# Moving vector-engine work in a transformer kernel: the context half's low parts, and the scalings of four attention heads

## What is computed

```
# end of the first block: the embedding gate
e = sigmoid(x @ w_ple_gate) * (p @ w_ple_proj)
x = x + rmsnorm(e, ple_post_norm)

# start of the second block, layer 0
xn = modulate(rmsnorm_2(h,  norm_mix), sh_m,  sc_m)     # latent half, h = x
xc = modulate(rmsnorm_2(hc, norm_mix), csh_m, csc_m)    # context half
# differential attention over both halves, per head
p = softmax(q1 k1) - lam * softmax(q2 k2);  o = p @ v
o = rmsnorm_2(o, subln) * (1 - lam_init);   y = o @ wo
```

## Time and profile before

| | before |
|---|---|
| median of 3 runs | 1462.05 us |
| profiled execution | 1463.88 us |
| its span | 1462.1 us |
| PE busy | 1411.9 us (97%) |
| DVE busy | 707.8 us (48%) |
| ACT busy | 610.8 us (42%) |
| POOL busy | 854.7 us (58%) |

### The profile page before, as it was taken

The page is one execution under the profiler, slowest core; times in us unless marked ns, Lnnn a source line. Parts: engine busy times, 40 slices in busy tenths (PEclk is TensorE's granted clock), DMA queues, the critical chain, the costliest instruction groups (busy, mean ns, idle before and its releaser), DMA issues.

```text
span 1462.1 us, 25892 instructions
## 1 busy us (share of the span) xinstructions
PE 1411.9 (97%) x9196; PEld 1262.4 (86%) x9196; DVE 707.8 (48%) x1315; ACT 610.8 (42%) x976; POOL 854.7 (58%) x426
## 2 busy tenths in 40 slices
PE   8999999999899999699999999999999999999998
PEld 7998999999787888577888888888888788999997
DVE  5884555555625556635655655334324383311111
ACT  6346544544533444534322322322332265444452
POOL 4785688798455766241443543544374452688895
PEclk8999999999899999899999999999999999999999
DMA  7653477785322223021565565635293101455563
GB/s 292 228 151 123 177 269 273 283 303 190 123 87 69 76 73 102 1 91 54 201 209 191 178 213 183 217 130 175 69 263 114 45 5 64 135 185 184 176 210 106
DMA packets 82971, 227.27 MB, mean 155 GB/s; under 512 B 23648, under 2 KB 29024, under 8 KB 82656
## 3 DMA queue, kind: packets, MB, share of 16 engines
q1 hardware_dynamic: 82464, 224.91, 45.6%
q10 hardware_dynamic: 448, 1.57, 0.5%
HBM read 222.26 MB, written 1.05 MB: 153 GB/s over the span
## 4 chain that ended last, share of the span: by engine, by line
issue 36%; PE 32%; POOL 27%; DVE 2%; ACT 1%; POOLq 1%; DVEq 0%; ACTq 0%
POOL wl L528 24%; PE ps L1045 7%; PE ps L1047 7%; PE ps L1046 7%; PE ps L1118 1%; PE ps L1132 1%; PE ps L1108 1%; PE ps L1109 1%; PE ps L1110 1%; PE ps L1382 1%; POOL xl L562 1%; PE ps L1308 1%; PE ps L1329 1%; PE ps L1396 1%; PE ps L1374 1%
## 5 line engine op out<-in xcount | busy, mean ns | idle before, releaser
L528 POOL TENSOR_TENSOR wl<-raw,wh 128x1024 fp32r<-128x1024 f32 x310 | 743.4, 2419 | 542.0 <-ACT wh L632 541.9
L1045 PE MATMUL ps<-xh,wh 128*128 128x256 f32 (+1 forms) x1728 | 561.4, 325 | 10.5 <-POOL wl L528 2.9
L1046 PE MATMUL ps<-xl,wh 128*128 128x256 f32 (+1 forms) x1728 | 555.1, 321 | 0.0
L1047 PE MATMUL ps<-xh,wl 128*128 128x256 f32 (+1 forms) x1728 | 554.8, 321 | 0.0
L632 ACT ACTIVATE wh<-raw 128x1024 fp32r<-128x1024 f32 x310 | 318.2, 1053 | 283.4 <-PE ps L1047 194.7
L1045 PEld LDWEIGHTS ps<-xh,wh 128*128 128x128 f32 x1728 | 330.7, 191 | 43.7 <-POOL wl L528 5.2
L1047 PEld LDWEIGHTS ps<-xh,wl 128*128 128x128 f32 x1728 | 330.5, 191 | 24.1
L1046 PEld LDWEIGHTS ps<-xl,wh 128*128 128x128 f32 x1728 | 330.9, 191 | 22.4
L1045 PE MATMUL ps<-fh,wh 128*128 128x256 f32 (+1 forms) x528 | 168.8, 320 | 1.7 <-POOL wl L528 1.7
L1046 PE MATMUL ps<-fl,wh 128*128 128x256 f32 (+1 forms) x528 | 168.6, 319 | 0.0
L1047 PE MATMUL ps<-fh,wl 128*128 128x256 f32 (+1 forms) x528 | 168.6, 319 | 0.0
(11 more groups left out here) (223 smaller groups left out, 1663.3 us busy)
## 6 DMA issues: line engine op xcount, KB each, us to landing
raw<-wall SPq DMA_DIRECT2D x310, 512.0 KB, 3.7
ada_late<-wada SPq DMA_DIRECT2D x56, 512.0 KB, 3.4
ada<-wada SPq DMA_DIRECT2D x40, 512.0 KB, 3.7
bias<-rpb SPq DMA_DIRECT2D x16, 256.0 KB, 6.2
h<-xin SPq DMA_DIRECT2D x2, 1024.0 KB, 7.2
sww<-qk SPq DMA_DIRECT2D x16, 128.0 KB, 2.3
csb<-cond SPq DMA_DIRECT2D x1, 1024.0 KB, 8.2
sw<-u ACTq DMA_DIRECT2D x2, 512.0 KB, 6.7
```

Source lines behind the costliest of these rows:

```text
L528: nc.gpsimd.tensor_tensor(wl[:, slot, :, :], raw[:, slot, :, :], wh[:, slot, :, :].bitcast(F32), ALU.subtract).then_inc(lo_ready, 1)
L1045: nc.tensor.matmul(o, wa, xa, start=start, stop=False, skip_group_check=True)
L1046: nc.tensor.matmul(o, wa, xb, start=False, stop=False, skip_group_check=True)
L1047: return nc.tensor.matmul(o, wb, xa, start=False, stop=stop, skip_group_check=True)
```

## The change

It moves DVE's instructions alone; the other four engines' programs are the same.

```diff
                 V.tensor_tensor(ppo[:, 2 * p:2 * p + 2, :], ppo[:, 2 * p:2 * p + 2, :], pair_banks(p % 2, SEQ), ALU.mult)\
                     .then_inc(bank_free, 1)
-                modulate_part(0, 1, CTX_TILES[p] if p < 3 else (), CTX_TILES[p - 1] if p else (), yc)
+                modulate_part(0, 1, CTX_TILES[p] if p < 3 else (), {1: CTX_TILES[0], 3: CTX_TILES[1]}.get(p, ()), yc)
             recip("ple1", SEQ)
             add_normed(ppo, par_ap("ple_post"))
+            modulate_part(0, 1, (), CTX_TILES[2], yc)
...
-                    def out_scaled(b):
+                    def out_scaled(b, tiles):
...
-                        dve.wait_ge(S("da_root"), b + 1)
-                        link(V.reciprocal(part, part))
-                        link(V.tensor_scalar(part, part, 1.0 - LAM_INIT, None, ALU.mult))
-                        for t in range(4):
+                        if 0 in tiles:
+                            dve.wait_ge(S("da_root"), b + 1)
+                            link(V.reciprocal(part, part))
+                            link(V.tensor_scalar(part, part, 1.0 - LAM_INIT, None, ALU.mult))
+                        for t in tiles:
...
                         combine(w)
-                        if w == 16:
-                            out_scaled(0)
                     for w in range(WOVEN, ATT0 + 5):
...
+                        if WOVEN < w <= WOVEN + 4:
+                            out_scaled(0, (w - WOVEN - 1,))
                         if w - 5 >= WOVEN:
                             squares(w - 5)
 
                     out_low(0)
-                    out_scaled(1)
+                    out_scaled(1, range(4))
```

## The result

The changed kernel took 1455.51 us (median of 6 runs, 1452.23 to 1458.34) against 1462.74 us before (6 runs). The measured ratio is 0.9944, 95% interval 0.9931 to 0.9956, so 8.2 us less; it is not the quotient of the two medians, which lie 7.2 us apart. A second set of runs later gave 1453.24 us and 0.9925 (0.9912 to 0.9938), 11.0 us less (10.4 by the medians). The forecast was 8.75 us less and 1453.3 us. The span of the profiled execution went from 1462.1 to 1453.1.

The account below looks back on a forecast made before the run. PE was taken to be bound by two waits for DVE, 4.82 us in the gate and 6.83 us in the attention. A -3.15 and B -5.6 sum to -8.75: 1462.05 to 1453.3 us, range 1449.8 to 1457.9.

Parts of the forecast that it names:

- A: Gate: DVE's add for the sum of squares starts earlier, PE's sums follow; -3.15 us, bounds -2.5 and -4.5.
- B: Attention: the sum of B1 to B4, -5.6 us.
- The clock, which I had as a rival with 0.18: Gate: granted clock stays high behind the shorter idle, A becomes -4.5, 1452.0 us in all; chance 0.18.
- B1: Attention: group 17's maxima start at once after its scores, so its turn comes earlier; -6.6 us, bounds -6.8 and -5.5.
- B2: Attention: without PE's long idle, group 17's turn and scores run at a higher clock; -1.2 us, bounds -1.2 and 0.
- B3: Attention, group 18: a small DVE instruction on the chain may wait for POOL; +0.65 us, bounds 0 and +1.3.
- B4: Last six groups: moved work costs 3.0 us less 1.45 us of idle; +1.55 us, bounds 0 and +3.0.
- the clock in the last groups: Rival: clock stays low over all six last groups as PE waits longer; +3.2 us, 1465.2; chance 0.03.
- The weights: Rival: the weight stream sets the pace behind the gate, A and part of B go; about 1461 us; chance 0.04.

Follow-up runs that it names:

- e1: Gate's part of the change alone, attention as before, against the kernel before: 0.9969, -4.5 us.
- e2: Attention's part of the change alone, gate as before, against the kernel before: 0.9973, -3.9 us.
- e5: Kernel before plus 30 filler matmuls on PE ahead of the sums of the gate's norm, DVE's order old: 0.9994 of before.
- e8: Changed kernel with e3's and e4's rearrangements and a second filler between the columns of the norm m0's sums: 0.9898 of before, 1448.80 us.
- e10: Changed kernel with e3's and e4's rearrangements together, a repeat run of that kernel: 0.9906 of before.
- e4: Changed kernel with the four scalings of heads 0 to 3 in steps 24 to 27 instead of 19 to 22: 0.9921 of before.
- e3: Changed kernel with the copy of the last projection pair ahead of group 18's maxima instead of behind them: 0.9920 of before.
- e9: Changed kernel with filler matmuls on PE ahead of its wait for the combines of groups 18, 19 and 22: 0.9916 of before.
- e6: Changed kernel with all scalings of heads 0 to 3 in step 17, behind group 17's maxima: 0.9959 of before.
- e11: e8's kernel with e9's fillers in the last groups added: 0.9906 of before, 1450.62 us.

## Why the prediction came out as it did

The time was right, and both mechanisms are shown: each of the two long waits of PE went (to 1.58 and 0.81 us), and each part alone gives its share (e1, e2). That the number came so near is in part luck: A came out 1.4 us larger than forecast in the two profiles compared above and B 2.0 us smaller, and the granted clock is behind much of both.

*A, the gate.* The order gave 3.25 us (product of pair 1 to the add: 14.64 before, 11.39 after) where I had 3.15. The clock, which I had as a rival with 0.18, held high in this place and added 1.82 at the reciprocal; e5 gives the same 1.83 by itself, though its time did not fall with it. Of the 11 profiles with the changed gate 9 show it; e8 and e10 reach the reciprocal at 16.48 and 16.77 us instead of 15.4. At the reciprocal of the norm m0 the gain was 5.51 us, of which 0.9 was given back by group 16's turn: layer 0's first products now ran in a low stretch (394.5 to 401.4). From the one profile before, A is -4.58 to -4.98 in ten of the 11 profiles and -3.05 in e10, not -3.15; and e2, with the old order, is itself 1.2 us longer than that profile.

*B1.* The maxima of group 17 came 6.64 us earlier (-6.6 forecast). From their start to the end of the combine it took 7.45 us and not 6.83, mostly because one small instruction (L1820) took 1.20 us beside POOL (0.34 before); the turn came 6.01 earlier.

*B2.* Turn and scores at the high clock: -1.15 (-1.2 forecast).

*B3* was off in size: +1.28 instead of +0.65. The wait that I forecast came as forecast: L1804 took 0.77 us beside POOL instead of 0.17, and e4, which has the same order here and a high clock, is 0.60 longer than before (4.22 against 3.62). The other 0.68 is a term that I left out: the clock fell at 585.7, and from the start of group 19's scores to its maxima it took 1.69 us, in e4 1.01. The copy L1793, for which PE idled 2.17 us, is not a cost of its own. It stood behind the small instruction before, too; PE now only came to wait for it earlier. It can be taken out of the way, as e3 shows.

*B4:* +2.23 instead of +1.55. The products took 0.68 to 0.69 us each, as forecast. The idle time of 1.45 us that I set against 3.0 us of work was still there in part (0.77 before group 22's maxima): the wait for scores moved along with the chain. And part of the 2.23, up to 0.9 by e9, is the clock again; e4 takes back the whole, scalings and clock together.

B was -3.65 and not -5.6; A and B together -8.2 and not -8.75. I had the clock in the last groups only as a rival in which it stays low over all six, and no term for its falling over a part of them, as it did in the changed kernel (585.7 to 589.1 and 592.5 to 599.3). The weights took nothing back, and no low part was late.

## What to carry to other kernels

An engine's instruction is not to be priced by its own row alone: DVE's four products took 6.15, 4.42 and 2.50 us, by whether POOL was at work beside them, so work without a deadline is best moved to where the other engine rests (e6 against the changed kernel), and then to where its own engine idles (e4). Idle time in a loop that feeds itself is only partly there to be filled: look for it in the loop's last steps, where e4 put the scalings (2.8 us for the products alone) and the stretch stayed at 24.24 us. An idle time of PE costs twice if the clock falls with it; count what runs behind it at both levels. But do not take such a gain as time won before the time shows it: e5 had 1.83 us of it in the gate's profile and none in its median ratio (0.9994).

## What the runs showed of the hardware

DVE instructions with one operand in PSUM ran at their usual length beside POOL (L1511, 0.86 us for two at 380.93; L1603, 0.43). The low part L1518, with its tensors in SBUF, took 2.25 us beside POOL at 382.85 and 0.47 with POOL idle (in the kernel before, at 379.75). Small instructions from SBUF to SBUF can be held as well: the scaling of 16 numbers per partition (L1842) took 2.07 us beside POOL and 0.17 without.

The granted clock stayed high over the gate's sums behind an idle of 1.6 us in 9 of 11 profiles and was low over them behind 4.8 us in both profiles with the old order and no fillers in the idle time (before and e2). Over the sums of the norm m0, with one filler between the columns, it fell for 6.8 us in all nine profiles of the changed gate that have one.

The spread between executions of one kernel was 6.1 us in the first set of the changed kernel, 2.4 in the second, and 2.1 and 0.25 in the two kernels with fillers in the last groups (5 runs each). So only the 0.25 of e11 stands out, and that the clock is its cause isn't shown: only the profiled executions show where it fell.
